# A fourth early gate panel and a spread chain of small products in the delta stage of a two-model kernel on one core

## The reference

```python
def gated_deltanet_mixer(x, w_in, conv_w, a_log, dt_bias, norm_w, w_out):
    proj = x @ w_in                       # 4096 columns of q, k, v; 2048 of z; 2 x 16 of gates
    qkv, z, b, a = jnp.split(proj, ...)
    qkv = jax.nn.silu(causal_depthwise_conv(qkv, conv_w))          # 4 taps
    ...                                   # l2norm of q and k, beta and g from b and a
    o = chunk_gated_delta_rule(...)       # 16 heads
    o = rms_norm(o) * norm_w
    o = o * jax.nn.silu(z...)
    return o.reshape(...) @ w_out

def chunk_gated_delta_rule(q, k, v, g, beta):
    ...
    a = jnp.where(strict, einsum(k_beta, k) * decay, 0.0)
    t_inv = triangular_solve(eye + a, eye)                          # the inverse of each chunk
    u, w = t_inv @ v_beta, t_inv @ (k_beta * exp(g))
    def step(state, inp):                                           # chunk by chunk
        v_new = u_n - w_n @ state
        o = q_g_n @ state + qk_n @ v_new
        state = state * exp(gl_n) + k_tail_n^T @ v_new
```

## Time and profile before

| what | value |
|---|---|
| median of 3 runs | 1987.55 us (1983.15 to 1987.73) |
| the profiled execution | 1986.61 us, span 1984.8 us |
| PE busy | 1956.2 us, 99% of the span |
| DVE, ACT, POOL busy | 70%, 55%, 6% |
| granted TensorE clock over the span | 0.995 |
| delta stage | about 1501 to 1788 us of the span |

### The profile page before, as it was taken

One profiled execution on the slowest core, in us unless ns is written; L12 is line 12 of the kernel. 1 busy time (PEld: TensorE's weight loads), 2 busy tenths in 40 slices (PEclk: granted clock), 3 DMA queues, 4 the chain that ended last, 5 costly groups with the idle time before them and its releaser, 6 DMA issues.

```text
span 1984.8 us, 41590 instructions
## 1 busy us (share of the span) xinstructions
PE 1956.2 (99%) x15610; PEld 1823.6 (92%) x15610; DVE 1397.1 (70%) x2394; ACT 1101.6 (55%) x1845; POOL 122.0 (6%) x204
## 2 busy tenths in 40 slices
PE   8999999999999999999999999999999899999998
PEld 7999899989999999999999999999999899989998
DVE  6688877766788877666667765575557978477655
ACT  5665555556654655554454544454447878556443
POOL 2031000000040000000000000000000333000000
PEclk9999999999999999999999999999999899999999
DMA  9433665544335555465546455555554544445552
GB/s 313 151 128 128 222 208 189 187 171 149 129 122 187 204 188 187 151 213 190 190 154 216 149 203 190 186 173 190 184 189 162 184 123 134 151 159 199 185 188 95
DMA packets 118248, 348.49 MB, mean 176 GB/s; under 512 B 23336, under 2 KB 35960, under 8 KB 117744
## 3 DMA queue, kind: packets, MB, share of 16 engines
q1 hardware_dynamic: 115392, 335.23, 49.4%
q0 software_dynamic: 2736, 11.59, 1.8%
HBM read 340.81 MB, written 5.96 MB: 175 GB/s over the span
## 4 chain that ended last, share of the span: by engine, by line
PE 89%; DVE 5%; ACT 4%; issue 1%; DMA 0%; SPq 0%; DVEq 0%; ACTq 0%
PE bank L2420 28%; PE bank L2422 27%; PE bank L2421 27%; DVE wlo L1603 1%; ACT whi L1024 1%; PE bank L2734 1%; ACT xhi L1040 1%; DVE arena L1671 1%; DVE conv L2134 1%; PE bank L2456 1%; PE bank L2707 0%; ACT psq L1048 0%; PE bank L2926 0%; PE bank L2695 0%; DVE xlo L1614 0%
## 5 line engine op out<-in xcount | busy, mean ns | idle before, releaser
L2420 PE MATMUL bank<-xhi,whi 128*128 128x256 f32 x3368 | 958.2, 285 | 7.1 <-DVE wlo L1603 3.0
L2421 PE MATMUL bank<-xlo,whi 128*128 128x256 f32 x3368 | 943.5, 280 | 1.1 <-issue 1.1
L2422 PE MATMUL bank<-xhi,wlo 128*128 128x256 f32 x3368 | 942.9, 280 | 0.0
L1603 DVE TENSOR_TENSOR wlo<-raw,whi 128x1024 fp32r<-128x1024 f32 x621 | 750.5, 1231 | 199.6 <-ACT whi L1024 196.9
L2420 PEld LDWEIGHTS bank<-xhi,whi 128*128 128x128 f32 x3368 | 635.3, 189 | 21.1 <-DVE wlo L1603 4.0
L2421 PEld LDWEIGHTS bank<-xlo,whi 128*128 128x128 f32 x3368 | 635.9, 189 | 7.0 <-issue 1.3
L1024 ACT ACTIVATE whi<-raw 128x1024 fp32r<-128x1024 f32 x621 | 632.4, 1045 | 12.3 <-DMA raw<-panels 6.6
L2422 PEld LDWEIGHTS bank<-xhi,wlo 128*128 128x128 f32 x3368 | 635.3, 189 | 0.0
L2420 PE MATMUL bank<-whi,hhi 128*128 128x512 f32 x688 | 272.8, 396 | 0.5 <-DVE hlo L1794 0.5
L2422 PE MATMUL bank<-whi,hlo 128*128 128x512 f32 x688 | 271.0, 394 | 0.0
L2421 PE MATMUL bank<-wlo,hhi 128*128 128x512 f32 x688 | 270.3, 393 | 0.0
(11 more groups left out here) (393 smaller groups left out, 1744.2 us busy)
## 6 DMA issues: line engine op xcount, KB each, us to landing
raw<-panels SPq DMA_DIRECT2D x621, 512.0 KB, 3.6
arena<-w_in POOLq DMA_DIRECT2D x2, 2048.0 KB, 10.5
arena<-relay SPq DMA_DIRECT2D x8, 512.0 KB, 5.5
arena<-gains_in POOLq DMA_DIRECT2D x6, 512.0 KB, 4.0
relay<-arena POOLq DMA_DIRECT2D x4, 512.0 KB, 8.2
relay<-arena SPq DMA_DIRECT2D x4, 512.0 KB, 3.5
x<-x_in SPq DMA_DIRECT2D x1, 1024.0 KB, 5.0
arena<-bias_table POOLq DMA_DIRECT2D x8, 128.0 KB, 7.4
```

Source lines behind the costliest of these rows:

```text
L1603: dve.tensor_tensor(wlo[slot][:], raw[slot][:], whi[slot][:].bitcast(F32), ALU.subtract) \
L2420: pe.matmul(dst, w_hi, a_hi, start=start, stop=False, skip_group_check=True)
L2421: pe.matmul(dst, w_hi, a_lo, start=False, stop=False, skip_group_check=True)
L2422: return pe.matmul(dst, w_lo, a_hi, start=False, stop=stop, skip_group_check=True)
```

## The change

A fourth gate panel becomes early and takes slot 11, directly behind the first set's last tile (slot 10). All tiles of sets 1 to 3 come one slot later; one gate panel fewer stands behind the last tile, and the stage still has 47 slots. Steps of set 0's chain keep their slots, since they count from slot 10. The early panel's result needs 256 floats more per partition in the arena.

`AMID` is dropped. `CHAIN` now holds for each step a slot and a half, `MIDDLE` or `END`, on all three engines. In sets 0 to 2 the lowest levels are drawn apart. The square roots for the output norm come a slot later, and the output heads are scaled in two slots instead of three.

```diff
-Z, EARLY_Z = 15, 3
+Z, EARLY_Z = 15, 4
-Z_AT = {3: 0, 6: 1, 9: 2, **{LAST + f: f for f in range(EARLY_Z, Z)}}
+Z_AT = {3: 0, 6: 1, 9: 2, 11: 3, **{LAST + f: f for f in range(EARLY_Z, Z)}}
-CHAIN = ({"w16": 13, "t16": 13, "u16": 14, "w32": 14, "t32": 14, "w64": 15, "u64": 16, "r0": 17, "s1": 18, "ks": 19,
-          "r1": 20, "o": 21},
-         {"w16": 12, "t16": 12, "u16": 13, "w32": 13, "t32": 14, "w64": 15, "u64": 16, "r0": 17, "s1": 18, "ks": 19,
-          "r1": 20, "o": 21},
...
-AMID = (("w16", "u16", "w32"), ("w16", "u16"), ("w16", "u16"), ("w16", "u16", "w32", "w64", "s1"))
+MIDDLE, END = 0, 1
+LATER = {"u64": (16, END), "r0": (17, END), "s1": (18, END), "ks": (19, END), "r1": (20, END)}
+SPREAD = {"w16": (12, MIDDLE), "t16": (13, MIDDLE), "u16": (13, END), "w32": (14, MIDDLE), "t32": (15, MIDDLE),
+          "w64": (15, END), **LATER, "o": (22, MIDDLE)}
+CHAIN = ({"w16": (13, MIDDLE), "t16": (14, MIDDLE), "u16": (14, END), "w32": (14, END), "t32": (15, MIDDLE),
+          "w64": (15, END), **LATER, "o": (22, MIDDLE)},
+         SPREAD, {**SPREAD, "t16": (12, END), "u16": (13, MIDDLE), "o": (21, END)},
+         {"w16": (12, MIDDLE), "t16": (12, END), "u16": (13, MIDDLE), "w32": (13, MIDDLE), "t32": (13, END),
+          "w64": (14, MIDDLE), "u64": (14, END), "r0": (15, END), "s1": (16, MIDDLE), "ks": (16, END), "r1": (17, END),
+          "o": (18, END)})
-ROOT_AT = 43
+ROOT_AT = 44
-SCALED_AT = {44: (0, 1), 45: (2, 3), 46: (4, 5)}
+SCALED_AT = {45: (0, 1, 2), 46: (3, 4, 5)}
```

PE's new function, which is called with `MIDDLE` between the halves of a panel and with `END` behind it; DVE and ACT have theirs with the copies:

```diff
+            def delta_chain(n, o, half):
+                here = lambda step: CHAIN[n][step] == (o - late(n), half)
+                if here("w16"):
+                    delta_w16(n)
+                if here("t16"):
+                    delta_t16(n)
...
+                if here("o"):
+                    delta_o(n)
```

More of the change, by code:

```diff
@@ L2337, in delta_o_scaled, with delta_chain @@
                                       .to_broadcast([P, nk, P]), ALU.mult).then_inc(d["o_scaled"], 1)
+            def delta_chain(n, o, half):
+                here = lambda step: CHAIN[n][step] == (o - late(n), half)
+                if here("w16"):
+                    delta_w16(n)
+                if here("t16"):
+                    delta_t16(n)
+                if here("u16"):
+                    delta_u16(n)
+                if here("w32"):
+                    delta_w32(n)
+                if here("t32"):
+                    delta_u32(n)
+                if here("ks"):
+                    delta_v1_in(n)
             def delta_step(s, n, o):
@@ L2352, in delta_step @@
                     delta_qmat(n)
-                if p == CHAIN[n]["t16"]:
-                    delta_t16(n)
-                if p == CHAIN[n]["w32"] and "w32" not in AMID[n]:
-                    delta_w32(n)
-                if p == CHAIN[n]["t32"]:
-                    delta_u32(n)
-                if p == CHAIN[n]["ks"]:
-                    delta_v1_in(n)
-                if p == 23 and n + 1 < SETS:
+                delta_chain(n, o, END)
+                if p == CHAIN[n]["o"][0] + 2 and n + 1 < SETS:
                     delta_o_added(n)
@@ L2368, in delta @@
                     for n in range(SETS):
-                        p = set_step(t, n) - late(n)
-                        if p == CHAIN[n]["w16"]:
-                            delta_w16(n)
-                        if p == CHAIN[n]["u16"]:
-                            delta_u16(n)
-                        if p == CHAIN[n]["w32"] and "w32" in AMID[n]:
-                            delta_w32(n)
+                        delta_chain(n, set_step(t, n), MIDDLE)
                     if t in TILE_AT and t != 2:
@@ L2840, in delta_amid @@
                 for n in range(SETS):
-                    p = set_step(t, n) - late(n)
-                    if p == CHAIN[n]["w16"]:
-                        delta_w16(n)
-                    if p == CHAIN[n]["u16"]:
-                        delta_u16(n)
-                    if p == CHAIN[n]["w32"] and "w32" in AMID[n]:
-                        delta_w32(n)
-                    if p == CHAIN[n]["w64"] and "w64" in AMID[n]:
-                        delta_w64(n)
-                    if p == CHAIN[n]["s1"] and "s1" in AMID[n]:
-                        delta_s1(n)
+                    delta_chain(n, set_step(t, n), MIDDLE)
             def delta_rows(s, n):
@@ L3046, in delta_o, with delta_chain @@
                         last.then_inc(d["o_sum"], 1)
+            def delta_chain(n, o, half):
+                here = lambda step: CHAIN[n][step] == (o - late(n), half)
+                if here("w16"):
+                    delta_w16(n)
+                if here("t16"):
+                    delta_t16(n)
+                if here("u16"):
+                    delta_u16(n)
+                if here("w32"):
+                    delta_w32(n)
+                if here("t32"):
+                    delta_t32(n)
+                if here("w64"):
+                    delta_w64(n)
+                if here("u64"):
+                    delta_u64(n)
+                if here("r0"):
+                    delta_r0(n)
+                if here("s1"):
+                    delta_s1(n)
+                if here("ks"):
+                    delta_ks(n)
+                if here("r1"):
+                    delta_r1(n)
+                if here("o"):
+                    delta_o(n)
             def delta_step(s, n, o):
@@ L3062, in delta_step @@
                     delta_turn_v(n, p - 9)
-                if p == CHAIN[n]["t16"]:
-                    delta_t16(n)
-                if p == CHAIN[n]["w32"] and "w32" not in AMID[n]:
-                    delta_w32(n)
-                if p == CHAIN[n]["t32"]:
-                    delta_t32(n)
-                if p == CHAIN[n]["w64"] and "w64" not in AMID[n]:
-                    delta_w64(n)
-                if p == CHAIN[n]["u64"]:
-                    delta_u64(n)
-                if p == CHAIN[n]["r0"]:
-                    delta_r0(n)
-                if p == CHAIN[n]["s1"] and "s1" not in AMID[n]:
-                    delta_s1(n)
-                if p == CHAIN[n]["ks"]:
-                    delta_ks(n)
-                if p == CHAIN[n]["r1"]:
-                    delta_r1(n)
-                if p == CHAIN[n]["o"]:
-                    delta_o(n)
+                delta_chain(n, o, END)
             def delta(s):
```

38 lines of the change are left out of this document (13 added, 25 removed).

## The result

The changed kernel takes 1994.03 us (median of 8 runs, 1991.09 to 1997.92) where the kernel before, run beside it, takes 1985.56 us (8 runs, 1981.98 to 1987.73). The ratio is 1.0049, 95% interval 1.0038 to 1.0060: slower by 7.5 to 12 us. The forecast was 1988, inside the 0.3% that it counted as no change.

A forecast was written before the change was run, and what follows sets the result against it. PE, busy 99%, was taken as the bound, so only its waits and clock count. 0.7 + 1.3 - 1.2 - 0.5 = +0.3 us on 1986.61 gave 1986.9; the higher median made it 1988 us, range 1981 to 1994.5 (8 in 10).

The forecast's parts named there:

- Set 0, +0.7: First set's chain: 2.8 us gained at full clock, 3.5 us lost to a clock fall about 1580; bounds -2.8 and +7.
- rival 2: Set 0: ACT's stop makes the clock fall at the key products' wait, +7 instead of +0.7, 1994.5 us; chance 0.12.
- The prediction's own sign of being wrong: Set 0: wrong if the solve ends well before 1565, DVE's copies come early, or clock stays 1.00 through 1577 to 1591.
- Set 1, +1.3, bounds -1.5 and +4.7: New wait ahead of set 0's output products, +2.8, less issue gap 1.0 and tmp wait 0.5; upper bound if clock falls.
- rival 3: Second clock fall at set 0's output products, +3.4 us, about 1992 to 1994 us; chance 0.12.
- Set 2, -1.2: Set 1's output products stand half a panel further behind u16, so their wait of 1.2 us goes; issue gap stays.
- Set 3, 0, and the end, -0.5: Set 3's issue gap of 1.5 us stays; at the end, last output products cover the 0.5 us wait for hlo.

The follow-up runs named there:

- e3: Changed kernel with set 0's output products half a panel later, at the end of their slot; 1991.16 us, 1.0035 of the kernel before.
- e4: Changed kernel with t32 of sets 1 and 2 half a panel earlier, at the end of w32's slot; 1987.73 us, 1.0020 of the kernel before.
- e2: Changed kernel without the fourth early gate panel, keeping the new table of the chain's half slots; 1986.40 us, 1.0015 of the kernel before.
- e14: e13 with set 0's output products put back to the middle of slot 22; 1983.17 us, 1.0000 of the kernel before.
- e10: Changed kernel with e3's and e4's edits, gate panel in slot 15 (overwrites a key tile), set 2's t16, u16 and set 1's outputs later; 1977.37 us, 0.9966.
- e13: e12 with set 2's t16 and u16 and set 1's output products half a panel later; 1980.07 us, 0.9979 of the kernel before.
- e12: e6 with set 0's turned blocks ahead of set 1's decay in their slot; 1981.36 us, 0.9989 of the kernel before.
- e5: Changed kernel with set 0's turned blocks one slot later on ACT, behind set 1's decay; 1990.94 us, 1.0034 of the kernel before.
- e6: Changed kernel with the edits of e3, e4 and e5 together; 1981.62 us, 0.9987 of the kernel before.

## Why the prediction was wrong

The sum was +0.3 us. The profile gives +5.1, the medians 8.5. The step that failed is set 1: w64's wait for ACT's copy was put at nothing, and the clock's fall at the output products was kept out of the sum. By its own terms:

- *Set 0, +0.7.* Measured -1.3 (-1.9, of which 0.6 were there ahead of the chain). The reading of ACT was right: it stood 5.1 us (4 forecast), the silu came about 1568, PE waited 3.25 (2.4 forecast), nothing at the DMA. Of the waits of 1.6, 1.9 and 2.0 us ahead of t16, w32 and t32 0.45, 1.4 (gap and copy) and 1.6 came. The fall did not come about 1580 for 10 us but at the key products, and for 3.5 us, in this execution. This is rival 2's fall without its price; in the profiles of e3 and e4 there is a second one from 1589. The prediction's own sign of being wrong came true: the clock stayed at 1.00 from 1577 to 1591. That -1.3 lies near +0.7 is partly luck, since a shorter fall and shorter waits made up for an earlier fall. POOL's solve, which the prediction thought might end 0.3 to 0.75 us earlier, ended 0.3 later (1565.6 for 1565.3).
- *Set 1, +1.3, bounds -1.5 and +4.7.* Measured +7.1, out of its bounds, and here the prediction failed. The wait ahead of the output products was right (2.93, forecast 2.6 to 3.0) and the clock fell there, which the forecast held only as a bound and as rival 3, at the price given (3.4). But w64 was costed at nothing. The prediction listed DVE's copies between the small products, and for ACT's t32 copy had no line: half a panel from t32 to w64 against ACT's table load and silu ahead of that copy. e4 shows that this pair of waits, one in set 1 and one in set 2, was the largest loss that a single edit took back, 4.4 to 5.8 us with its clock. Rivals 2 and 3 named times (1994.5, 1992 to 1994) close to the measured 1994.03, but neither had this wait, and rival 2's price of 7 us in set 0 was not paid; that their numbers fit is luck.
- *Set 2, -1.2.* Measured +2.4. The wait of the output products went as forecast. Again a w64 wait (1.48) with a fall behind it, and an issue gap of 1.9 instead of 1.1.
- *Set 3, 0, and the end, -0.5.* Measured -1.7, and -0.8 at the end. The fall of 3.4 us that before's profile had at 1701 wasn't there; the gap of 1.5 at t16, which was forecast to stay, went, and one of 0.7 at w32 and a DMA wait of 0.4 came.

The wider failure is in the clock. The prediction put one fall into the sum, in set 0, and left the other places out of it; against an early fall it held that set 2 once stood 2.3 us in 8.2 without one. In all 16 profiles every half-clock stretch of the stage begins within a stop of PE of 1.1 us or more, or less than 4 us after its end, and behind the same stop it comes in some executions and not in others. So each stop should have been given a share of a fall: over all kernels here, from 11.3 to 19.1 us of idle, a line through ratio and idle gives 1.8 us of time for 1 us of idle (e2 lies 4 to 5 us above it). With that, even the idle that was forecast (+3.2 in set 0, +1.3 in set 1, -1.2 and -0.5, 2.8 us) means 5 us, and with w64's 2.9 of waits 10.

The Trainium skill (TensorE: Matmul & The Clock Gate, What's actually happening) says that how many matmuls run at the low clock differs from run to run of one kernel. The runs here agree: 0.993 to 0.999 for the kernel before.

## What to carry to other kernels

When a step is moved by half a slot, write down for each product that waits on another engine which instructions stand ahead of the copy on that engine, for every set and every engine; here the one engine left out was the one that cost most. On a kernel that PE bounds, price a stop of PE at more than its length, since the clock often falls behind it: 1.8 times over all kernels here, 1.4 to 1.9 times in e14, about once in e3. One profile shows only one draw of that; the mean granted clock over many runs tells more. Where small products come in bursts, look in the trace for gaps without a releaser at fixed counts of instructions, and give the group ahead of one more dense work. When a spreading that is right in principle comes out slow, look for the two or three half slots that it made too narrow before giving it up: three edits took 11 us off the changed kernel, which put it 2.6 us ahead of the kernel it came from, and two more brought that to 4 us.

## What the runs showed of the hardware

- The idle gaps with no releaser stand at fixed places of PE's instruction order, whatever product is there. Two rows of before, then one of the changed kernel:

```profile
1581.55 0.75 PE L2971 MATMUL bank<-arena 32*32 32x32 f32 x21 [1.04 <-issue]
...
1661.76 0.39 PE L2421 MATMUL bank<-xlo,whi 128*128 128x256 f32 x1 [1.08 <-issue]
```

```profile
1582.97 0.17 PE L2946 MATMUL bank<-arena 32*16 32x16 f32 x1 [1.03 <-issue]
```

The first row's gap stands ahead of PE's 11,922nd matmul, in w32; that of the changed kernel is ahead of the 11,922nd too, which is now in u16. All 16 profiles have a gap there, 0.7 to 3.1 us long. If a trace's weight loads, matmuls and sequencer instructions of PE are counted in the order of their starts, all 46 such gaps of 0.25 us or more in the stage (16 profiles) fall at a count that leaves 53 or 54 when divided by 256. They come where the 256 instructions ahead were issued fast: of 46 such groups in the chain that took 2.7 to 3.7 us, 45 have a gap (0.3 to 3.1 us, of quite different length for the same instructions), and of 294 slower ones (5.0 us or more) one has, of 0.3. This is what the spreading does to them: set 2's group of 3.7 us takes 5.0 in e10, e13 and e14, and its gap is gone in all three; set 1's went from 2.7 us before to 6.4 in the changed kernel, and its gap of 1.0 went with it. Only e4 lost a gap with its group as fast as ever. What PE does in a gap no trace names. The Trainium skill (Runtime: NRT & Kernel Launch, Instruction fetch mechanics) has instructions fetched in blocks of 256 and the cost of a block's boundary mostly hidden; the spacing of the gaps agrees with the first, and if they are fetch, up to 3 us of it here are not hidden.
- The profiles of before and after lost the same 8.5 us of granted clock in the stage, in one piece of 13.7 us and one of 3.4 before, in four pieces after. Not all of a lost clock is paid: 0.001 of a span of 1985 us is 2.0 us, and goes with 1.35 us of time among the runs of one kernel. That the rest lies under waits is likely, but not shown.
- GpSimd's solve sets how early the first inverse can come. It ends at 1565.3 before, 1565.6 in the changed kernel and 1566.2 in e12, and the way from the end of ACT's copy of the blocks through the relay to w16 took 5.3 (e5, e6), 5.5 (before) and 6.3 us (e12). Freeing ACT brings the blocks no earlier than the solve ends.
